# Fourteen projection tiles of the RWKV mixer as seven pairs of seven half-width products

## What is computed

```python
h = rms_norm_2(x, norm_mix[l])
p_rw, p_s5, p_gla, p_gate = _split_2(h @ w_in[l], IN_SIZES)     # 1792, 512, 1552, 3072 columns
y_rw  = rwkv7_mix(p_rw, ...)      # begins with: p = p + (_token_shift(p) - p) * mu
y_s5  = s5_mix(p_s5, ...)         # ends with:   y = y * sigmoid(y @ w_glu + b_glu), y = gelu(...)
y_gla = gla_mix(p_gla, ...)       # chunked gated linear attention
...
def rwkv7_mix(p, mu, w0, w_up, a0, a_up, g_up, ...):
    p = p + (_token_shift(p) - p) * mu
    r, k, v, wd, ad, gd = _split_2(p, RWKV_SIZES)               # 512, 512, 512, 64, 64, 128
    w_log = -softplus(-(w0 + tanh(wd) @ w_up)) - 0.5
    a = sigmoid(a0 + ad @ a_up)
    g = sigmoid(gd) @ g_up
    ...
```

## Time and profile before

| | us |
|---|---|
| median of three runs | 2867.88 |
| lowest and highest | 2867.54 and 2868.18 |
| span of the profiled execution | 2867.8 |
| stretch of S5, 1561 to 1693 | 132 |
| stretch of GLA beside RWKV, 1693 to 1832 | 139 |
| TensorE busy in the span | 2825.6 (99%) |

### The profile page before, as it was taken

One profiled execution on the slowest core, in us unless ns is written; L12 is line 12 of the kernel. 1 busy time (PEld: TensorE's weight loads), 2 busy tenths in 40 slices (PEclk: granted clock), 3 DMA queues, 4 the chain that ended last, 5 costly groups with the idle time before them and its releaser, 6 DMA issues.

```text
span 2867.8 us, 37205 instructions
## 1 busy us (share of the span) xinstructions
PE 2825.6 (99%) x15288; PEld 1954.7 (68%) x15288; DVE 1551.9 (54%) x3162; ACT 649.2 (23%) x1343; POOL 5.0 (0%) x22
## 2 busy tenths in 40 slices
PE   8999999999999999999999999999999999999998
PEld 3567588888544575888886545455555875688887
DVE  5685544453336874556736753455443533666654
ACT  5651310010135613101001031422120102222200
POOL 0000000000000000000000000000000000000000
PEclk9999999999999999999999999999999999999999
DMA  4013122232221132222222121211112321222222
GB/s 148 30 51 104 52 94 84 85 105 89 82 72 48 56 103 81 80 84 87 89 95 89 60 67 59 74 39 46 46 52 94 115 94 51 81 88 89 88 89 81
DMA packets 61944, 223.78 MB, mean 78 GB/s; under 512 B 6992, under 2 KB 7248, under 8 KB 61264
## 3 DMA queue, kind: packets, MB, share of 16 engines
q1 hardware_dynamic: 61776, 221.42, 23.6%
HBM read 219.29 MB, written 2.10 MB: 77 GB/s over the span
## 4 chain that ended last, share of the span: by engine, by line
PE 95%; DVE 4%; issue 1%; DMA 0%; ACT 0%; SPq 0%; DVEq 0%
PE ps L1728 29%; PE ps L695 18%; PE ps L1135 15%; PE ps L1123 9%; PE ps L1204 4%; PE ps L1510 3%; PE ps L1483 2%; PE ps L1166 2%; PE ps L1495 2%; PE ps L2213 1%; PE ps L2234 1%; PE ps L2434 1%; PE ps L3105 1%; PE ps L1809 1%; DVE shaped L1599 1%
## 5 line engine op out<-in xcount | busy, mean ns | idle before, releaser
L1135 PE MATMUL ps<-h,ring 128*128 128x512 f32 x752 | 346.3, 603 | 0.0
L1728 PE MATMUL ps<-h,ring 128*128 128x256 f32 x1136 | 269.0, 380 | 3.9 <-ACT q_p L1764 2.0
L1728 PEld LDWEIGHTS ps<-h,ring 128*128 128x128 f32 x1136 | 214.9, 190 | 37.8 <-issue 8.7
L1135 PEld LDWEIGHTS ps<-h,ring 128*128 128x128 f32 x752 | 136.1, 189 | 148.2 <-issue 142.8
L1728 PE MATMUL ps<-h_sums,w_sums 128*128 128x256 f32 x1008 | 224.4, 379 | 0.0
L1728 PEld LDWEIGHTS ps<-h_sums,w_sums 128*128 128x128 f32 x1008 | 191.5, 190 | 26.0
L695 PE MATMUL ps<-hid_sums,d_sums 128*128 128x256 f32 x720 | 171.1, 379 | 0.5 <-DVE hid_sums L1687 0.5
L695 PEld LDWEIGHTS ps<-hid_sums,d_sums 128*128 128x128 f32 x720 | 136.7, 190 | 19.4 <-issue 0.8
L1669 DVE TENSOR_TENSOR d_sums<-ring 128x512 f32<-128x512 f32 (+1 forms) x48 | 31.5, 655 | 174.1 <-DMA ring<-stream_dram 164.3
L1204 PE MATMUL ps<-o_x,ring 128*128 128x512 f32 x256 | 112.2, 593 | 0.0
L1728 PE MATMUL ps<-c_h_sums,c_sums 128*128 128x256 f32 x504 | 112.2, 379 | 0.0
(11 more groups left out here) (647 smaller groups left out, 4662.2 us busy)
## 6 DMA issues: line engine op xcount, KB each, us to landing
ring<-stream_dram SPq DMA_DIRECT2D x394, 512.0 KB, 3.6
bias<-bias_dram SPq DMA_DIRECT2D x8, 448.0 KB, 4.7
mem<-mem_dram SPq DMA_DIRECT2D x3, 1024.0 KB, 6.0
out_dram<-x SPq DMA_DIRECT2D x8, 256.0 KB, 2.2
x<-x_dram SPq DMA_DIRECT2D x3, 512.0 KB, 8.2
rope_ab<-ropes_dram SPq DMA_DIRECT2D x4, 256.0 KB, 7.8
s_big<-s_big_dram SPq DMA_DIRECT2D x1, 1024.0 KB, 7.0
constants<-constants_dram SPq DMA_DIRECT2D x1, 768.0 KB, 11.3
```

Source lines behind the costliest of these rows:

```text
L1135: mm = pe.matmul(out, w, r, start=(k == 0), stop=(k == len(rhs) - 1))
L1728: mm = pe.matmul(ps[:, bank + at, 0:256], w(k), x(k), start=start and k == 0, stop=k == 3, skip_group_check=not start)
```

## The change

The 14 tiles are formed as seven pairs by `two_steps`: products P1, P6, P7, P5, P2, P4, P3, each of four matmuls with 256 columns, in two banks of 512 columns (even pairs in banks 6 and 7, odd pairs in 4 and 5): P1 and P6 in the halves of the first, P7 and P5 in the halves of the second, then P2 on P1, P4 on P7, P3 on P5. Between them stand waits: P6 for the sums s1, s2, s3 of the weights (`two_sums`, VectorE), P2 for `u` = P1 + P6, P4 for both `v` = u + P7 and c22 = v + P5, P3 for s4. ScalarE copies P1 and c11 (`two_act`), VectorE makes the five combinations (`two_dve`) and the two token mixes of the pair. A pair's first two units must both have landed before its sums are made. The four sums of h, each 128 x 1024, are made once, in S5 after step q = 9. The RWKV columns begin at a whole unit of the stream. One pair stands before the S5 output and six after it. ScalarE's tanh now waits for GLA's last product too (`g_fin`). The `residual` strand is due at 40.4 + 5 k.

```diff
+    def two_steps(self, pe, i, unit, sums, ts, banks):
...
+        p1, p6 = (a, lo, lambda k: half(top, k), lambda k: h[:, k, lo]), (a, hi, sk(1), tk(1))
+        p7, p5 = (b, lo, sk(2), tk(2)), (b, hi, sk(0), tk(0))
+        p2 = a, lo, lambda k: half(top, 4 + k), lambda k: h[:, 4 + k, lo]
+        p4 = b, lo, lambda k: half(bottom, 4 + k), tk(3)
+        p3 = b, hi, sk(3), lambda k: h[:, 4 + k, hi]
+        for u in (unit, unit + 1):
+            pe.wait_ge(self.arrived[u % RING], 16 * (u // RING + 1))
+        for n, (bank, part, w, x) in enumerate((p1, p6, p7, p5, p2, p4, p3)):
+            if n == 1:
+                pe.wait_ge(*s['w_s2'].at(i + 1))
+            if n == 4:
+                pe.wait_ge(*s['w_u'].at(3 * i + 1))
+            if n == 5:
+                pe.wait_ge(*s['w_u'].at(3 * i + 3))
+            if n == 6:
+                pe.wait_ge(*s['w_s4'].at(i + 1))
+            for k in range(4):
+                mm = pe.matmul(ps[:, bank, part], w(k), x(k), start=n in (0, 2) and k == 0, stop=k == 3, skip_group_check=True)
+                if k == 3:
+                    mm.then_inc(*s['w_p'].up())
+                elif n == 0 and k == 0:
+                    self.unit_done(mm, unit)
+                elif n == 6 and k == 1:
+                    self.unit_done(mm, unit + 2)
...
+                if k % 2:
+                    yield
...
+    def two_sums(self, dve, i, unit, sums, part):
...
+        if part == 0:
+            for u in (unit, unit + 1):
+                dve.wait_ge(self.arrived[u % RING], 16 * (u // RING + 1))
+            if i:
+                dve.wait_ge(*s['w_p'].at(7 * i - 3))
+            dve.tensor_tensor(s1, a21, a22, ALU.add).then_inc(*s['vec'].up())
+            first = s['vec'].now()
+            dve.tensor_tensor(s3, a11, a21, ALU.subtract).then_inc(*s['vec'].up())
+            dve.wait_ge(*first)
+            dve.tensor_tensor(s2, s1, a11, ALU.subtract).then_inc(*s['w_s2'].up())
...
+                    if q == 9:
+                        dve.wait_ge(*s['prepared'].now())
+                        self.rhs_sums(dve, self.h_sums)
...
-                    for n in range(14):
-                        yield 10 + 6.85 * n if n < 2 else 24 + 6.85 * n
...
+                    for part in range(2):
+                        self.two_sums(dve, 0, self.shift_units[0], sums, part)
+                    for i in range(pairs):
...
+                        yield max(begin(i) + 3.9, 6.5)
+                        combine(0)
+                        yield begin(i) + 7
+                        combine(1)
+                        if i + 1 < pairs:
+                            yield begin(i) + 7.3
+                            self.two_sums(dve, i + 1, self.shift_units[i + 1], sums, 0)
+                        yield begin(i) + 12.2
+                        combine(2)
...
-            self.low_mixed = [s['mixed'].at(13), s['mixed'].at(14)]
+            self.low_mixed = [s['mixed'].at(13), s['mixed'].at(14), s['g_fin'].at(4)]
```

More of the change, by code:

```diff
@@ L190, in put_second_block @@
     w.put(pack_columns(np.concatenate([up] * 4), seq(0, 256)))
+    w.align(UNIT_BLOCKS)
     w.put(pack_columns(m, seq(r0, 256)))
@@ L885, in pe @@
                         pe.wait_ge(*s['f_sig'].at(gate - 1))
-                    elif k == 0 and gate == 1:
-                        pe.wait_ge(*net.shift_read[1])
+                    elif k == 0:
+                        for read in net.shift_read[5 + 2 * gate]:
+                            pe.wait_ge(*read)
                     next(side)
@@ L1734, in products_up @@
         self.unit = first + 2 * i + 3
+    def two_steps(self, pe, i, unit, sums, ts, banks):
+        s, ps, h = self.s, self.ps, self.h
+        top, bottom = self.ring[:, unit % RING, :], self.ring[:, (unit + 1) % RING, :]
+        half = lambda w, k: w[:, k * P:(k + 1) * P]
+        lo, hi = slice(0, 256), slice(256, 512)
+        a, b = banks
+        sk = lambda j: (lambda k: half(sums[:, j, :], k))
+        tk = lambda j: (lambda k: ts[:, j, k, :])
+        p1, p6 = (a, lo, lambda k: half(top, k), lambda k: h[:, k, lo]), (a, hi, sk(1), tk(1))
[22 more added lines that the diff above has]
+                    self.unit_done(mm, unit + 2)
+                if k == 3 and n == 6:
+                    self.block_at, self.unit = (unit + 2) * UNIT_BLOCKS, unit + 1
+                if k % 2:
+                    yield
@@ new lines, in two_sums @@
+    def two_sums(self, dve, i, unit, sums, part):
+        s = self.s
+        top, bottom = self.ring[:, unit % RING, :], self.ring[:, (unit + 1) % RING, :]
+        a11, a12, a21, a22 = top[:, 0:512], top[:, 512:1024], bottom[:, 0:512], bottom[:, 512:1024]
+        s1, s2, s3, s4 = (sums[:, j, :] for j in range(4))
+        if part == 0:
[8 more added lines that the diff above has]
+            dve.tensor_tensor(s2, s1, a11, ALU.subtract).then_inc(*s['w_s2'].up())
+        else:
+            dve.wait_ge(*s['w_s2'].at(i + 1))
+            if i:
+                dve.wait_ge(*s['w_p'].at(7 * i))
+            dve.tensor_tensor(s4, a12, s2, ALU.subtract).then_inc(*s['w_s4'].up())
@@ L2382, in pe_ @@
                     pe.wait_ge(*self.gla_read)
+                if m == 4:
+                    for read in self.shift_read[5]:
+                        pe.wait_ge(*read)
                 if m >= 5:
@@ L3311, in shifted @@
                 def shifted():
[L3312 to L3317, removed]
+                    for i in range(pairs):
+                        yield begin(i) + 3.5
+                        self.two_act(act, i, p1[:, :], None, banks(i), 0)
+                        yield begin(i) + 8.7
+                        self.two_act(act, i, None, pr[:, slot(2 * i), lo], banks(i), 1, s['mixed'].at(2 * i - 2) if i >= 2 else None)
                 def gates():
```

118 lines of the change are left out of this document (87 added, 31 removed).

## The result

The changed kernel takes 2874.83 us (median of ten runs, 2873.24 to 2876.28), the kernel before 2867.68 (ten runs, 2867.18 to 2868.41): ratio 1.0023, 95% interval 1.0015 to 1.0031, or +7.15 us. The prediction said 2869.7 with a range to 2873.5, so the time lies outside, on the slower side.

The account below looks back on a forecast made before the run. TensorE, busy 99% of the span, was taken to bound the kernel. -11.5 - 0.5 + 1.5 + 4.9 + 2.6 + 4.8 = +1.8 us on 2867.8 gave 2869.7 us, range 2864.5 to 2873.5.

Parts of the forecast that it names:

- TensorE's products and the old stop: 196 half-width matmuls replace 112 full ones, -11.5 us; the 0.54 us idle before the first attention product goes, -0.5 us.
- sums of h: Four VectorE instructions in S5 delay step q = 10, absorbed before TensorE needs anything: 0, other end 1.2 us.
- wait 1: Before P2 of pair 0, TensorE waits for u, as ScalarE's copy of P1 comes late: +1.5 us.
- wait 2: Before the third S5 output, TensorE waits for GLA's sigmoid, held up behind VectorE's sums of pair 1: +4.9 us.
- wait 3: Before P2 and P4 of the last pair, VectorE's mixes and root tiles delay u and c22: +0.7 and +1.9 us.
- pairs 1 to 4: P4 waits for v and c22, ready with 0.6 us to spare, so no stop of TensorE: 0.
- wait 4: Before the first product over `low_rw`, TensorE waits for `r_low`, whose tanh now waits for GLA's last products: +4.8 us.
- three signs: Prediction wrong if stage idle is under 6 us, idle appears in pairs 1 to 4, or half-width products exceed 0.44 us.
- The rival that reached as high: P4 also waits in pairs 1 to 4, behind GLA state steps: 2.8 to 5.6 us, 2872.5 to 2875.3; 15%.
- the one in which the waits do not form: Rival: ScalarE and VectorE catch up before TensorE asks, only the -12.0 us stays: 2855.9; 5%.
- some 7 us of idle: Expected in VectorE's timeline before the sums of pair 1, released by a load.
- The doubt about table loads: The Trainium skill adds a 1.38 us drain per ScalarE table load; waits 2 and 4 1.4 us longer each, sum +4.6.

Follow-up runs that it names:

- e7: Kernel before with only the four sums of h added in S5 after step q = 9, read by nobody: 2867.93 us.
- e1: Changed kernel with ten unread matmuls, five in each of TensorE's two long waits (S5 sigmoid, r_low): 2870.18 us.
- e4: Changed kernel with the edits of e2, e3 and e9 together: 2857.21 us, ratio 0.9962 to the kernel before.
- e2: Changed kernel with VectorE's sums of pair 1 due at 15.2, not 7.3, so behind GLA's gate: 2867.70 us.
- e3: Changed kernel with VectorE's list at the stage's end reordered and ScalarE's tanh waiting for the two mixes alone: 2866.29 us.
- e5: Kernel before with ten extra copies on ScalarE ahead of the tanh leading to r_low: 2874.56 us.
- e9: Changed kernel with ScalarE's copy of P1 of pair 0 due at 1.9, not 3.5, ahead of the gate's Exp: 2873.70 us.
- e8: Changed kernel with two unread matmuls in each of TensorE's two long waits, where e1 has five: 2873.43 us.
- e6: Kernel before with seven extra copies on ScalarE ahead of the tanh leading to r_low: 2872.09 us.

## Why the prediction was wrong

| step | forecast | measured |
|---|---|---|
| TensorE's products and the old stop | -12.0 | -12.2 |
| sums of h | 0 | 0 (e7: the same 126.22 us; median -0.1) |
| wait 1 | +1.5 | +1.40 |
| wait 2 | +4.9 | +4.90 |
| wait 3 | +0.7 and +1.9 | +0.65 and +1.90 |
| pairs 1 to 4 | 0 | 0 |
| wait 4 | +4.8 | +4.85 |
| clock behind waits 2 and 4 | not in the sum | +3.6 in the profiled execution, +4.9 in the median (e1) |
| not placed | | +0.8 |
| sum | +1.8 | +7.15 |

The terms of the right column come from traces, the clock and the sum from medians. The row "not placed" is what is missing between them, much the same as in e1 (+2.24, where the terms give +1.5) and in e4 (0.7).

**The step that failed** is the last one of the sum: "After wait 4 the next stage has the same order as before and starts as a block, so I carry no more." It starts as a block, but at the lower clock. The same was left out behind wait 2, where I went on at 0.8585 us for each matmul. That price, like all in the sum, is one at full clock, and it was applied to matmuls behind stops of a kind that the kernel before does not have in these stages. With the two falls, whose price only e1 gave, the forecast would have been 2869.7 + 4.9 = 2874.6, against 2874.83. That this is so close is partly luck: the products saved 0.2 us more than was taken, the waits came 0.1 us shorter, the kernel before was 0.2 us faster in these runs than where the forecast set out, and the 0.8 us that no trace places make up for it.

Of the three signs by which the prediction said it would know itself wrong, none appeared: the idle time was above 6 us, there was none in pairs 1 to 4, and a half-width product took 0.4318 us. A granted clock under 1.00 behind a stop was not among them, and no rival named it.

The trace of before did hold the warning, in a place that I did not read. At its very end, with TensorE's last matmul done, the windows show:

```profile
2855.00:2860.00 5.00, 1.52 (x6) 0.76 (x4) 2.64 (x4) 1.23 (x2) 0.00 (x0) 1.00 0.00 0
2860.00:2865.00 5.00, 0.00 (x0) 0.00 (x0) 4.96 (x9) 0.00 (x0) 0.00 (x0) 0.54 0.66 245
```

There is one block of matmuls behind a long idle stretch in it too, the first of the program:

```profile
8.24 9.80 PE L1123 MATMUL ps<-x_gained_ab,ring 128*128 128x512 f32 x16 [8.24 <-DMA ring<-stream_dram]
```

Its eight matmuls take 9.80 us where the next eight take 7.03. The clock column reads 1.00 there, so that this was the lower clock is not shown; but it was a price for a start after standing still, of the size that the falls then had. The kernel before has no other stop of over 1.2 us.

The range was too narrow for the same reason: it was made of the uncertainty of the waits, and these were all within 0.1 us. The rival that reached as high (P4 waiting in pairs 1 to 4) was wrong in its mechanism; there is no stop there. So was the one in which the waits do not form, though its time, 2855.9, is about what e4 reaches: 12 us were there to be had, with these waits taken out of the order.

**The waits were right, link by link.** Wait 2 in the timelines of VectorE and ScalarE, and wait 4 in the same two:

```profile
1708.24 0.69 DVE L1790 TENSOR_TENSOR rw_sums<-ring 128x512 f32<-128x512 f32 x1 [7.29 <-DMA ring<-stream_dram]
```
```profile
1715.05 1.28 ACT L3443 ACT_TABLE_LOAD   x1
1716.34 1.27 ACT L3443 ACTIVATE y_s<-ps,vectors 128x512 f32<-128x512 f32 x2
```
```profile
1827.56 2.49 DVE L3378 TENSOR_TENSOR y_gla<-y_gla,gla_go 128x512 f32<-128x512 f32 x4
```
```profile
1830.17 0.63 ACT L2492 ACTIVATE low_rw<-low_rw 64x512 f32<-64x512 f32 x1 [13.87 <-DVE y_gla L3378]
1830.82 1.28 ACT L2493 ACT_TABLE_LOAD   x1
1832.11 0.63 ACT L2493 ACTIVATE low_rw<-low_rw 128x512 f32<-128x512 f32 x1
```

VectorE sat 7.29 us before the sums of pair 1 ("some 7 us of idle" was the forecast), and ScalarE's tanh began when the last of GLA's products was done. The doubt about table loads is settled too: in both waits the sigmoid begins 0.01 us behind a load of 1.28, and with no drain the waits come out within 0.05 us of the sum; an extra 1.4 in each would have shown.

**A slip beside it.** I set the span of the profiled execution, 2867.8, beside the median of the times, 2867.88, and called them equal. In the later runs the time is 1.3 us above the span of the same execution, so the profiled one was about 1.2 us longer than the median; its second block of matmuls began at 18.74, the latest of the twelve traces. For a sum of differences this did no harm.

## What to carry to other kernels

Price a new stop of TensorE by what it does to the clock as well as by its length: two stops of 4.7 us cost 9.8 us themselves and 4.9 more behind them. An order written by due times has to be checked against what each engine's list waits for at that point; a few due times, GLA's last products put straight behind their root tiles, and one wait moved to the instructions that need it turned 7 us lost into 10.7 us gained, with the same arithmetic. Where a stop cannot be removed, matmuls that nobody reads can fill it (e1), though removing the stops gained more than three times as much here (17.9 against 4.9).

## What the runs showed of the hardware

- Behind a stop of 4.3 to 4.8 us every execution paid for at least one fall, by its time (the changed kernel, e2, e3, e5 and e9, nine to eleven executions each); with one of 2.42 us 6 of 11 did; with one of 1.80 us none for certain. Of two stops in one execution (e8) that of 2.97 us brought a fall and that of 3.09 none.
- The price of a fall was 1.7 to 3.2 us for eight matmuls of 128x512, and differed between executions. In the changed kernel, e9, e8 and e6 the clock fell between 0.1 us before and 0.7 us after the work began again, TensorE worked 3.3 to 3.4 us at 0.50, and the price was 1.7 or 1.8. In e5, e2 and e3 it fell 0.6, 1.3 and 1.8 us before the stop ended, TensorE worked 6.2, 5.6 and 5.0 us at 0.50, and the price was 3.2, 2.9 and 2.6. So it is about half of the time worked at the lower clock, and a trace with the low price alone understates the median (3.6 us in the changed kernel's, 4.9 by e1). Its four executions up to 2873.99 have a mean clock of 0.997, the six from 2874.76 on 0.996.
- Where a fall comes behind the stop, the windows inside the stop show nothing: in the changed kernel they read 1.00 and the first full window of work 0.50.
- A stop costs 0.16 us more than its idle time, since consecutive matmuls overlap by that much in the timeline: with no fall, eight matmuls of 128x512 take 7.03 us there and the next block begins 6.87 after them.
